# A feed-forward layer cut into four sections instead of two, with output groups between input groups, and 17 instead of 9 of 22 input groups done by seven block products

## The chip, the cores and the metric

The kernel runs on one core of one Trainium2 chip. The metric is the device time of one execution in microseconds (us). One execution was also recorded by the hardware profiler; every row shown below is from that one.

## The reference, cut to what matters

One inference step of a two-layer decoder trunk for 512 prompt tokens and 8 sample tokens (520 columns, D_MODEL 1024), all in float32. Four of its six phases are the same feed-forward half-step with weights of their own:

```python
D_FF = 2816
def swiglu(h, w_in, w_out):
    gate, up = jnp.split(h @ w_in, 2, axis=-1)
    return (jax.nn.silu(gate) * up) @ w_out
# x += 0.5 * swiglu(rms_norm(x), w_in, w_out)      four times: a0, b0, a1, b1
```

The other two phases are a retention/state-space mixer (between a0 and b0) and latent attention (between a1 and b1). The change touches only the four feed-forward phases.

## The kernel before, in words

**Split products.** Every float32 product is made of three matmuls in the reduced type: high part by high part, high by low, low by high. ScalarE makes the high part of a weight chunk (`split_high`, L356), VectorE the low part (`split_low`, L362), each 128 x 512. A chunk is one 256 KB load into a ring of four raw slots; the high and low parts have rings of four of their own. A raw slot is loaded again once its chunk's low part is done; a high slot is written again once TensorE has used the chunk that was there. All weight loads stand in one order on SyncE's queue.

**Input groups.** The 2816 hidden features are 22 groups g of 128. A plain group (`gemm`, L384) takes gate and up of 128 features: 4 chunks, 96 matmuls of 128 x 260. A group in `S_GROUPS` is done by `strassen` (L413 to L447): the product of a 2 x 2 block matrix in seven block products of 12 matmuls each, 84 in all. It needs four sums of weight blocks (`prepare` on VectorE: L910, L913, L914, L919, for which all four raw chunks of the group must have landed), their high and low parts (L662, L899), four sums of the activations made once in each phase (`t_sums` L882 to L887, their parts `t_highs` L652 and `t_lows` L894), and ScalarE copies of partial products out of PSUM (`copy_partial`, L657). TensorE waits inside the group: the third product for the first copy, the fifth for the third copy (`copied`), the seventh for VectorE's first half of `up_second` (L837, `evicted`). Then follow silu (L631), the product with up (L862), and the parts of the hidden tile (L639, L873).

**Output groups.** Each of four output groups (`gemm` on hidden tiles) adds into the residual (`residual`, L961).

**Order.** Two sections of 12 and 10 input groups; after each section its four output groups of 6 and 5 chunks (`mid` and `out`). Groups 0 to 3 are plain, then block-product and plain groups alternate, in hardware loops on TensorE, ScalarE and VectorE (`group_pair`). Accumulators alternate between two sets of four PSUM banks from step to step.

**The start of a phase.** While TensorE does group 0 and group 1, the norm's statistics are made: square root (L617), spread over the partitions by TensorE in the middle of group 1, and copied to `rstd` (L623), without which no group can be scaled out of PSUM. VectorE's list at the start (function `ffn` in the vector block) reads, cut:

```python
for g in range(FIRST_S - 1):
    splits(2 if g else 4)      # chunks of group g + 1
    if g == 0:
        stats((f, "in", 0), nn)
    gate_up(f, g)
    ...
    hidden_low(f, g)
    if g == 1:
        t_sums(f)
```

Each engine runs its list strictly in this written order and waits on semaphores; the order on each engine is written by hand.

Of the kernel before, what the change touches and what calls it, by code (L numbers as in the profile page):

```python
# [10 lines left out]
F32 = mybir.dt.float32  # L11
# [7 lines left out]
P = 128  # L19
# [23 lines left out]
R = 4  # L43
# [7 lines left out]
KFS = max(hi - lo for lo, hi in SECTIONS)  # L51
# [43 lines left out]
def ffn_steps(plan, f):  # L95
    for (lo, hi), name in zip(SECTIONS, ("mid", "out")):
        for g in range(lo, hi):
            plan.step((f, "in", g), 4)
        for g in range(4):
            plan.step((f, name, g), (hi - lo) // 2)  # L100
# [108 lines left out]
def program(nc, io, phases=PHASES):  # L209
# [181 lines left out]
    def count(eng, s, n, i=None, per=1):  # L391

        eng.wait_ge(s, n if i is None else per * i + n)

    def s_index(f, g):

        return len(S_GROUPS) * ffn_index[f] + S_GROUPS.index(g)

    def strassen(pe, f, g, i=None):


        step = (f, "in", g)
        acquire(pe, step, i)
        n, b0, j = plan.first[step], bank0(step), s_index(f, g)
        zb, yb, xb = b0, b0 + 1, b0 + 2

        def ring(c):
            count(pe, w_split, n + c + 1, i, 8)
            return WH[:, (n + c) % R, :], WL[:, (n + c) % R, :]

        def sums(s):
            count(pe, s_low, 3 * j + s + 1, i, 3)
            return SMH[:, s, :], SML[:, s, :]  # L413
# [20 lines left out]
        count(pe, copied, 3 * j + 1, i, 3)  # L434
        product(xb, sums(1), tsum(1), False).then_inc(product_done, 1)
        product(zb, ring(1), block(1, 0), True).then_inc(w_used, 1)
        count(pe, copied, 3 * j + 3, i, 3)
        product(xb, ring(2), tsum(2), False).then_inc(w_used, 1)
        product(yb, sums(2), block(1, 1), False).then_inc(product_done, 1)
        count(pe, evicted, 3 * j + 1, i, 3)  # L440
# [103 lines left out]
    def _(pe):  # L544
        def ffn(f):
# [4 lines left out]
            done = KF * ffn_index[f]  # L550
            h_rhs = lambda k: (HH[:, k, :], HL[:, k, :])
            for (lo, hi), name in zip(SECTIONS, ("mid", "out")):
                g0 = max(lo, FIRST_S)
                for g in range(2 if lo == 0 else lo, g0):
                    gemm(pe, (f, "in", g), 2, KD, x_rhs)
                if lo == 0:
                    pe.wait_ge(x_summed, 8 * (ffn_index[f] + 1))
                with pe.Fori(0, (hi - g0) // 2) as i:
                    strassen(pe, f, g0, i)
                    gemm(pe, (f, "in", g0 + 1), 2, KD, x_rhs, i, 8)  # L560
                for g in range(4):

                    gemm(pe, (f, name, g), 2, hi - lo, h_rhs,
                         before_k=(lambda k: pe.wait_ge(hl_done, done + lo + k + 1)) if g == 0 else None)
# [18 lines left out]
    def _(act):  # L583
# [35 lines left out]
        def stats(step, nn):  # L619
            roots(nn)  # L620
# [5 lines left out]
        def silu(f, g, i=None):  # L626
            if g in S_GROUPS:
                count(act, evicted, 3 * s_index(f, g) + 3, i, 3)
            else:
                wait_free(act, (f, "in", g), i)  # L630
            nc.scalar.activation(SGT[:, g % 2, :], GU[:, g % 2, 0, :], ACT.Silu).then_inc(silu_done, 1)  # L631

        def hidden_high(f, g, i=None):
            n = KF * ffn_index[f] + g + 1
            count(act, hid_done, n, i, 2)
            tile = g - (SECTIONS[1][0] if g >= SECTIONS[1][0] else 0)
            out = HH[:, tile, :] if i is None else HH[:, bass.ds(2 * i + tile, 1), :]
            src = HT[:, g % 2, :] if i is None else HT[:, g % 2:g % 2 + 1, :]
            nc.scalar.activation(out, src, ACT.Copy).then_inc(hh_done, 1)  # L639
# [14 lines left out]
        def copy_partial(f, g, i, bank, out, done, n, per):  # L654

            count(act, done, n, i, per)
            nc.scalar.activation(XU[:, out, :], PS[:, bank0((f, "in", g)) + bank, 0:TH], ACT.Copy).then_inc(copied, 1)  # L657

        def sum_high(f, g, s, i=None):

            count(act, s_sum, 4 * s_index(f, g) + (1, 2, 4)[s], i, 4)
            nc.scalar.activation(SMH[:, s, :], SR[:, s % 2 if s < 2 else 1, :], ACT.Copy).then_inc(s_high, 1)  # L662

        def prepare(f, g, i=None):

            n = plan.first[(f, "in", g)]
            high = lambda c: split_high(act, n + c, i, 6, 8, 2)
            high(0)
            sum_high(f, g, 0, i)
            sum_high(f, g, 1, i)  # L670
            high(1)
            count(act, s_sum, 4 * s_index(f, g) + 3, i, 4)
            high(2)
            sum_high(f, g, 2, i)

        def group_pair(f, g, i=None, before=True, after=True):


            n, j = plan.first[(f, "in", g)], s_index(f, g)
            high = lambda c: split_high(act, n + c, i, 6, 8, 2)  # L680
            high(3)
            copy_partial(f, g, i, 2, 0, w_used, plan.used_through(n), 6)
            if before:
                silu(f, g - 1, i)
            high(4)
            copy_partial(f, g, i, 1, 2, product_done, 3 * j + 1, 3)
            if before:
                hidden_high(f, g - 1, i)
# [2514 lines left out]
```

## Time and profile before

| | us |
|---|---|
| median of 3 runs (2270.8 to 2272.05) | 2271.09 |
| the profiled execution | 2268.74 |
| its span, first to last instruction | 2267.0 |
| TensorE busy | 2207.5 (97%) |
| VectorE busy | 1372.9 (61%) |
| ScalarE busy | 948.8 (42%) |

The profiled execution lies 2.35 us below the median of the runs, and 1.74 us of it lie outside the span. Matmuls are pipelined, so that TensorE is shown busy while it only drains; the distance between the starts of two matmuls is what one costs, not its duration. The names PE, PEld, DVE, ACT, POOL and SP in rows are TensorE's matmuls, its weight loads, VectorE, ScalarE, GpSimd and SyncE.

### The profile page before, as it was taken

What the parts mean: (1) busy time and instruction counts of PE and PEld (TensorE: products, weight loads), DVE (VectorE), ACT (ScalarE), POOL (GpSimd) and SP (SyncE); (2) the same over time, 40 slices, a digit from 0 to 9 for tenths busy, and PEclk for the clock granted to TensorE, in tenths of its full rate; (3) what the DMA queues carried; (4) which work ended last, traced back from release to release, by engine and by line L of the source; (5) the groups of instructions that cost most, each with busy time, mean ns of one, the idle gap of its engine ahead of it and who ended that gap; (6) DMA issues with size and microseconds to landing.
All of it is one profiled execution on the core that took longest, in us unless ns stands there. A gap on an engine that the chain in (4) does not pass through costs nothing.

```text
span 2267.0 us, 48608 instructions
## 1 busy us (share of the span) xinstructions
PE 2207.5 (97%) x19050; PEld 2125.9 (94%) x19050; DVE 1372.9 (61%) x2166; ACT 948.8 (42%) x1669; POOL 171.3 (8%) x243
## 2 busy tenths in 40 slices
PE   9999999999999999999999999999999989999997
PEld 9999999998888999999999999999996689999997
DVE  6754755787436547736746753765557747754754
ACT  6432433562324435423435432443346625432432
POOL 0000002022100010000001000001114501000001
PEclk9999999999999999999999999999999999999999
DMA  4333333233333232333332333333547822333332
GB/s 139 100 95 94 97 97 106 75 101 101 122 119 112 85 103 84 102 90 98 97 94 80 99 97 94 93 101 93 156 146 235 280 85 84 98 96 91 100 95 98
DMA packets 117591, 245.59 MB, mean 108 GB/s; under 512 B 15104, under 2 KB 15376, under 8 KB 116096
## 3 DMA queue, kind: packets, MB, share of 16 engines
q1 hardware_dynamic: 103248, 188.86, 27.6%
q0 software_dynamic: 14048, 54.49, 7.0%
q8 instruction: 111, 1.82, 0.3%
q14 instruction: 40, 0.33, 0.0%
q10 hardware_dynamic: 144, 0.09, 0.0%
HBM read 233.11 MB, written 9.95 MB: 107 GB/s over the span
## 4 chain that ended last, share of the span: by engine, by line
PE 86%; DVE 9%; ACT 2%; issue 2%; DMA 1%; SPq 0%; DVEq 0%; ACTq 0%
PE psum L384 63%; PE psum L428 5%; PE psum L427 5%; PE psum L429 5%; DVE w_low L362 2%; PE psum L2647 1%; PE psum L2662 1%; PE psum L1454 1%; DVE gate_up L827 1%; ACT w_high L356 1%; DVE conv_sum L1884 1%; PE psum L2734 1%; DVE probs_by_key L3074 1%; PE psum L2632 0%; PE psum L2692 0%
## 5 line engine op out<-in xcount | busy, mean ns | idle before, releaser
L362 DVE TENSOR_TENSOR w_low<-w_raw,w_high 128x512 fp32r<-128x512 f32 x703 | 499.3, 720 | 462.2 <-ACT w_high L356 459.7
L356 ACT ACTIVATE w_high<-w_raw 128x512 fp32r<-128x512 f32 x703 | 435.0, 627 | 689.4 <-PE psum L384 533.9
L384 PE MATMUL psum<-x_high,w_high 128*128 128x260 f32 x2688 | 541.6, 283 | 9.3 <-DVE w_low L362 6.0
L384 PE MATMUL psum<-x_low,w_high 128*128 128x260 f32 x2688 | 537.8, 282 | 0.0
L384 PE MATMUL psum<-x_high,w_low 128*128 128x260 f32 x2688 | 537.7, 282 | 0.0
L384 PEld LDWEIGHTS psum<-x_high,w_high 128*128 128x128 f32 x2688 | 414.3, 188 | 16.4 <-issue 4.8
L384 PEld LDWEIGHTS psum<-x_high,w_low 128*128 128x128 f32 x2688 | 414.4, 188 | 0.0
L384 PEld LDWEIGHTS psum<-x_low,w_high 128*128 128x128 f32 x2688 | 414.3, 188 | 0.0
L384 PE MATMUL psum<-hidden_high,w_high 128*128 128x260 f32 x1408 | 282.7, 282 | 0.0
L384 PE MATMUL psum<-hidden_low,w_high 128*128 128x260 f32 x1408 | 282.7, 282 | 0.0
L384 PE MATMUL psum<-hidden_high,w_low 128*128 128x260 f32 x1408 | 282.7, 282 | 0.0
L384 PEld LDWEIGHTS psum<-hidden_high,w_high 128*128 128x128 f32 x1408 | 218.1, 188 | 0.0
L384 PEld LDWEIGHTS psum<-hidden_low,w_high 128*128 128x128 f32 x1408 | 218.1, 188 | 0.0
L384 PEld LDWEIGHTS psum<-hidden_high,w_low 128*128 128x128 f32 x1408 | 218.1, 188 | 0.0
L827 DVE TENSOR_TENSOR gate_up<-psum,rstd 128x520 f32<-128x520 f32 x104 | 67.8, 693 | 79.1 <-PE psum L384 64.8
L1062 POOL TENSOR_TENSOR square_sums<-squares 128x520 f32<-128x520 f32 x6 | 7.9, 1320 | 1415.0 <-ACT squares L607 1415.0
L873 DVE TENSOR_TENSOR hidden_low<-hidden,hidden_high 128x520 f32 (+1 forms) x88 | 61.5, 699 | 62.6 <-ACT hidden_high L639 62.6
L662 ACT ACTIVATE w_sums_high<-w_sums 128x512 fp32r<-128x512 f32 x108 | 67.8, 628 | 63.3 <-DVE w_sums L910 53.8
L639 ACT ACTIVATE hidden_high<-hidden 128x520 f32 (+1 forms) x88 | 56.2, 639 | 87.3 <-DVE hidden L862 86.8
L427 PE MATMUL psum<-x_sums_high,w_high 128*128 128x260 f32 x288 | 81.0, 281 | 8.1 <-ACT partial_products L657 8.1
L961 DVE SCALAR_TENSOR_TENSOR residual<-psum,residual 128x1040 f32<-128x1040 f32 x39 | 48.4, 1241 | 65.5 <-PE psum L384 64.1
L631 ACT ACTIVATE silu_gate<-gate_up 128x520 f32<-128x520 f32 x88 | 55.4, 630 | 77.0 <-DVE gate_up L827 76.7
(438 smaller groups left out, 3510.2 us busy)
## 6 DMA issues: line engine op xcount, KB each, us to landing
w_raw<-in_weights_dram SPq DMA_DIRECT2D x704, 256.0 KB, 2.6
cache_pages<-in_cache_pages_dram POOLq DMA_DIRECT2D x128, 272.0 KB, 4.3
ret_sample_state<-in_state_ret_dram POOLq DMA_DIRECT2D x2, 2048.0 KB, 7.5
out_ret_s_dram<-ret_sample_state POOLq DMA_DIRECT2D x2, 2048.0 KB, 6.6
out_y_dram<-residual SPq DMA_DIRECT2D x8, 260.0 KB, 2.2
ssm_sample_state<-in_state_ssm_dram POOLq DMA_DIRECT2D x2, 1024.0 KB, 5.3
out_ssm_s_dram<-ssm_sample_state POOLq DMA_DIRECT2D x2, 1024.0 KB, 4.8
residual<-in_x_dram SPq DMA_DIRECT2D x3, 520.0 KB, 7.0
```

The costliest lines, as they stand in the source:

```text
L356: nc.scalar.activation(WH[:, slot, :], WRAW[:, slot, :], ACT.Copy).then_inc(w_high, 1)
L362: nc.vector.tensor_tensor(WL[:, slot, :], WRAW[:, slot, :], WH[:, slot, :].bitcast(F32), ALU.subtract).then_inc(w_split, 1)
L384: mm = nc.tensor.matmul(PS[:, b0 + 2 * m + half, 0:cols], w, x[:, half * cols:(half + 1) * cols], start=start, stop=stop)
L427: nc.tensor.matmul(PS[:, bank, 0:TH], wh, xh, start=fresh and kp == 0, stop=False, skip_group_check=True)
L428: nc.tensor.matmul(PS[:, bank, 0:TH], wh, xl, start=False, stop=False, skip_group_check=True)
L429: mm = nc.tensor.matmul(PS[:, bank, 0:TH], wl, xh, start=False, stop=kp == 3, skip_group_check=True)
L631: nc.scalar.activation(SGT[:, g % 2, :], GU[:, g % 2, 0, :], ACT.Silu).then_inc(silu_done, 1)
L639: nc.scalar.activation(out, src, ACT.Copy).then_inc(hh_done, 1)
L662: nc.scalar.activation(SMH[:, s, :], SR[:, s % 2 if s < 2 else 1, :], ACT.Copy).then_inc(s_high, 1)
L827: ins = nc.vector.tensor_tensor(out[:, 2 * m:2 * m + 2, :], acc(step)[:, 2 * m:2 * m + 2, :], halves(RSTD[:]), ALU.mult)
L873: nc.vector.tensor_tensor(out, src, hi.bitcast(F32), ALU.subtract).then_inc(hl_done, 1)
L961: nc.vector.scalar_tensor_tensor(x, acc(step), scale, x, ALU.mult, ALU.add).then_inc(acc_free[plan.set_of[step]], 1)
```

## The change

Four sections of 6, 6, 6 and 4 groups. All groups but 0, 1, 2, 3 and 5 are done by block products (17 of 22). The output groups of a section ("out a", "out b", "out c": 3 chunks each, "out": 2 chunks each) stand between the input groups of the next section; only the last four stand together at the end of the phase. Because output groups come four times instead of twice, there are 16 residual additions in a phase instead of 8. The loops are written out. Each step's side work (splits, sums, copies, evictions) is listed by two functions, `during_s` and `during_plain`, that take the step before, the current and the next one. At the start of a phase the scaling of x (`scaled`, L645) and the activation sums move to earlier places. With P for plain, S for block products, O for an output group, a phase is now: 0P 1P 2P 3P 4S 5P, then S O S S O S O S S O (groups 6 to 11), the same again (12 to 17), S O S O S O S O (18 to 21), O O O O.

```diff
-SECTIONS = ((0, 12), (12, 22))
-FIRST_S = 4
-S_GROUPS = [g for lo, hi in SECTIONS for g in range(max(lo, FIRST_S), hi, 2)]
+SECTIONS = ((0, 6), (6, 12), (12, 18), (18, 22))
+OUT_NAMES = ("out a", "out b", "out c", "out")
+PLAIN_GROUPS = (0, 1, 2, 3, 5)
+S_GROUPS = [g for g in range(KF) if g not in PLAIN_GROUPS]
...
+    order = inner(0, 1, 2, 3, 4, 5)
+    for s in (0, 1):
+        a = SECTIONS[s + 1][0]
+        order += inner(a) + out(s, 0) + inner(a + 1, a + 2) + out(s, 1) + inner(a + 3) + out(s, 2)
+        order += inner(a + 4, a + 5) + out(s, 3)
+    for g in range(4):
+        order += inner(18 + g) + out(2, g)
+    return order + [(f, "out", g) for g in range(4)]
...
 # ScalarE
+        def during_s(prev, cur, nxt):
+            late = kind(prev) == "S"
+            if late:
+                splits(1)
+                silu(prev)
+                copy_product1(cur)
+                split_a21(cur)
+                hidden_high(prev)
+                copy_product5(cur)
+                splits(1)
+                copy_products16(cur)
+                sum_high(cur, 2)
+                splits(3)
+                return
+            splits(1)
+            copy_product1(cur)
+            splits(1)
+            if kind(prev) == "P":
+                silu(prev)
+            copy_product5(cur)
+            if kind(prev) == "P":
+                hidden_high(prev)
+            copy_products16(cur)
+            if kind(nxt) == "S":
+                sum_high(nxt, 0)
+                sum_high(nxt, 1)
+            else:
+                splits(3 if kind(nxt) == "P" else 2)
+        def during_plain(prev, cur, nxt):
+            if prev:
+                silu(prev)
+            splits(1)
+            if prev:
+                hidden_high(prev)
+            sum_high(nxt, 0)
+            sum_high(nxt, 1)
+            splits(1)
+            sum_high(nxt, 2)
+            split_a21(nxt)
...
                 if g == 0:
-                    stats((f, "in", 0), nn)
+                    roots(nn)
+                    wait_stored(act, f)
+                    scaled(f, range(0, 4))
+                    spread(step, nn)
+                    scaled(f, range(4, 8))
                 if g == 1:
-                    scaled(f, range(0, 4))
-                if g == 2:
                     t_highs(f, 0, 1)
-                silu(f, g)
+                silu(step)
...
 # VectorE
+        def during_s(prev, cur, nxt):
+            late = kind(prev) == "S"
+            if late:
+                up_first(prev)
+                sum4(cur)
+                splits(1)
+                product(prev)
+                splits(1)
+                hidden_low(prev)
+                splits(1)
+                sum_low(cur, 2)
+                splits(2)
+                up_second(cur)
+                splits(1)
+                gate(cur)
+                return
+            splits(1)
+            if kind(prev) == "P":
+                gate_up(prev)
             else:
+                residual(prev, prev[2], 0.5)
+            if kind(nxt) == "S":
...
+                sums123(nxt)
+                splits(1)
+                sum_low(nxt, 0)
+                up_second(cur)
+                sum_low(nxt, 1)
+                gate(cur)
+                return
+            splits(1)
...
+            splits(1)
+            up_second(cur)
+            splits(1)
+            gate(cur)
...
+        def during_plain(prev, cur, nxt):
+            if prev:
+                if kind(cur) == "O":
+                    up_first(prev)
+                product(prev)
+            sums123(nxt)
+            splits(1)
+            if prev:
+                hidden_low(prev)
+            sum_low(nxt, 0)
+            sum_low(nxt, 1)
+            sum4(nxt)
+            splits(1)
+            sum_low(nxt, 2)
+            splits(1)
...
-            for g in range(FIRST_S - 1):
+            for g in range(3):
                 splits(2 if g else 4)
                 if g == 0:
-                    stats((f, "in", 0), nn)
+                    stats(step, nn)
-                gate_up(f, g)
-                if g == 2:
+                gate_up(step)
+                if g == 1:
                     t_lows(f, 0, 1)
...
-                hidden_low(f, g)
-                if g == 1:
+                hidden_low(step)
+                if g == 0:
                     t_sums(f)
-                if g == 2:
-                    t_lows(f, 3)
+                if g == 1:
+                    t_lows(f, 2, 3)
```

## Rows read from the trace of the kernel before

**Rows 1.** The page: busy time of each engine (share of the span, instructions).

```profile
PE 2207.5 (97%) x19050; PEld 2125.9 (94%) x19050; DVE 1372.9 (61%) x2166; ACT 948.8 (42%) x1669; POOL 171.3 (8%) x243
```

**Rows 2.** Timeline, phase a0, first matmuls of steps (start, length, engine, line, what).

```profile
71.23 0.40 PE L384 MATMUL psum<-x_high,w_high 128*128 128x260 f32 x2
82.75 0.28 PE L427 MATMUL psum<-x_high,w_high 128*128 128x260 f32 x1
92.73 0.40 PE L384 MATMUL psum<-x_high,w_high 128*128 128x260 f32 x2
147.25 0.40 PE L384 MATMUL psum<-hidden_high,w_high 128*128 128x260 f32 x2
216.37 0.28 PE L427 MATMUL psum<-x_high,w_high 128*128 128x260 f32 x1
```

**Rows 3.** Timeline of TensorE at the start of phase a1, waits in brackets.

```profile
1229.59 0.40 PE L384 MATMUL psum<-x_high,w_high 128*128 128x260 f32 x2
...
1241.66 0.47 PE L384 MATMUL psum<-x_high,w_high 128*128 128x260 f32 x2 [0.71 <-DVE w_low L362]
...
1254.13 0.39 PE L427 MATMUL psum<-x_high,w_high 128*128 128x260 f32 x1 [1.03 <-DVE w_low L362]
...
1257.47 0.38 PE L427 MATMUL psum<-x_sums_high,w_sums_high 128*128 128x260 f32 x1 [0.21 <-ACT partial_products L657]
...
1262.61 0.38 PE L427 MATMUL psum<-x_sums_high,w_high 128*128 128x260 f32 x1 [2.01 <-ACT partial_products L657]
```

**Rows 4.** Timeline of VectorE at the start of phase a1.

```profile
1225.25 0.70 DVE L862 TENSOR_TENSOR hidden<-silu_gate,gate_up 128x520 f32<-128x520 f32 x1 [0.70 <-ACT silu_gate L631]
...
1227.27 1.29 DVE L362 TENSOR_TENSOR w_low<-w_raw,w_high 128x512 fp32r<-128x512 f32 x2
...
1236.09 1.24 DVE L882 TENSOR_TENSOR x_sums<-x_scaled 128x1040 f32<-128x1040 f32 x1
...
1240.83 1.28 DVE L362 TENSOR_TENSOR w_low<-w_raw,w_high 128x512 fp32r<-128x512 f32 x2
```

**Rows 5.** Timeline of ScalarE at the start of phase a1.

```profile
1223.22 1.28 ACT L631 ACT_TABLE_LOAD   x1
1224.58 0.64 ACT L631 ACTIVATE silu_gate<-gate_up 128x520 f32<-128x520 f32 x1
...
1227.57 2.57 ACT L645 ACTIVATE x_scaled<-residual,vectors 128x520 f32<-128x520 f32 x4
```

**Rows 6.** Windows in the mixer phase, and one around the 2.01 us wait.

```profile
566.00:568.00 2.00, 0.00 (x0) 0.00 (x0) 1.93 (x4) 0.46 (x1) 0.60 (x2) 1.00 0.48 202
...
569.00:571.00 2.00, 2.00 (x5) 1.53 (x5) 1.25 (x2) 0.00 (x0) 0.00 (x0) 0.50 0.32 131
...
572.00:574.00 2.00, 2.00 (x18) 1.95 (x17) 0.00 (x0) 1.68 (x2) 0.55 (x1) 1.00 0.33 45
...
1260.00:1270.00 10.00, 7.99 (x68) 7.79 (x67) 7.07 (x12) 4.23 (x9) 0.00 (x0) 1.00 0.42 114
```

The columns are: the window, its length, busy time (and instructions) of PE, PEld, DVE, ACT and POOL, the granted clock (1.00 is 2.4 GHz, 0.50 is 1.2 GHz), the DMA share, GB/s.

**Rows 7.** Timeline: the first matmul after the idle stretch in the mixer phase.

```profile
568.71 1.22 PE L1364 MATMUL psum<-ssm_cum_rows,ssm_cum 128*128 128x512 f32 x2 [3.33 <-DVE ssm_x L2085]
```

**Rows 8.** VectorE: a landing after a split, and sums of a block-product group.

```profile
205.77 0.69 DVE L362 TENSOR_TENSOR w_low<-w_raw,w_high 128x512 fp32r<-128x512 f32 x1 [2.19 <-ACT w_high L356]
209.17 0.69 DVE L910 TENSOR_TENSOR w_sums<-w_raw 128x512 f32<-128x512 f32 x1 [2.71 <-DMA w_raw<-in_weights_dram]
...
210.57 0.69 DVE L914 TENSOR_TENSOR w_raw<-w_raw 128x512 f32<-128x512 f32 x1
211.17 0.68 DVE L362 TENSOR_TENSOR w_low<-w_raw,w_high 128x512 fp32r<-128x512 f32 x1
```

**Rows 9.** Groups by line: VectorE's half-width and widest instructions (count | busy, mean ns).

```profile
L837 DVE TENSOR_TENSOR gate_up<-psum,partial_products 128x260 f32<-128x260 f32 x36 | 15.4, 428 | 6.5 <-PE psum L429 6.3
...
L961 DVE SCALAR_TENSOR_TENSOR residual<-psum,residual 128x1040 f32<-128x1040 f32 x39 | 48.4, 1241 | 65.5 <-PE psum L384 64.1 <-PE psum L2734 1.4
```

**Rows 10.** DMA issues of the page: the slowest load on SyncE's queue (KB, us to landing).

```profile
residual<-in_x_dram SPq DMA_DIRECT2D x3, 520.0 KB, 7.0
```

More of the change, by code:

```diff
@@ L95, in ffn_steps @@
 def ffn_steps(plan, f):
[L96 to L100, printed above, removed]
+    for step in ffn_order(f):
+        lo, hi = SECTIONS[section_of(step)]
+        plan.step(step, 4 if step[1] == "in" else (hi - lo) // 2)
 def make_plan(phases):
@@ L549, in ffn, with pe_steps @@
             gemm(pe, (f, "in", 1), 2, KD, x_rhs, before_k=spread_at(pe, 3, (f, "in", 0), nn))
[L550 to L564, printed above, removed]
+            order = ffn_order(f)
+            pe_steps(order[2:])
+        def pe_steps(steps):
+            for step in steps:
+                f = step[0]
+                if kind(step) == "P":
+                    gemm(pe, step, 2, KD, x_rhs)
+                elif kind(step) == "S":
+                    if step[2] == S_GROUPS[0]:
+                        pe.wait_ge(x_summed, 8 * (ffn_index[f] + 1))
+                    strassen(pe, step)
+                else:
+                    lo, hi = SECTIONS[section_of(step)]
+                    t0, n0 = hidden_tile(lo), KF * ffn_index[f] + lo
+                    gemm(pe, step, 2, hi - lo, lambda k: (HH[:, t0 + k, :], HL[:, t0 + k, :]),
+                         before_k=(lambda k: pe.wait_ge(hl_done, n0 + k + 1)) if step[2] == 0 else None)
         pe.wait_ge(table_set, 2)
@@ L664, in prepare, with copy_product1 @@
[L664 to L688, printed above, removed]
-            copy_partial(f, g, i, 2, 1, product_done, 3 * j + 2, 3)
-            high(5)
-            high(6)
-            high(7)
-            silu(f, g, i)
-            hidden_high(f, g, i)
-            if after:
-                prepare(f, g + 2, i)
+        def copy_product1(step):
+            act.wait_ge(w_used, plan.used_through(plan.first[step]))
+            nc.scalar.activation(XU[:, 0, :], PS[:, bank0(step) + 2, 0:TH], ACT.Copy).then_inc(copied, 1)
@@ L900, in sum_low, with raw @@
                                     ALU.subtract).then_inc(s_low, 1)
-        def prepare(f, g, i=None):
-            n, j = plan.first[(f, "in", g)], s_index(f, g)
-            a11, a12, a21, a22 = (WRAW[:, (n + c) % R, :] for c in range(4))
-            loaded = lambda c: count(dve, w_loaded[(n + c) % R], 16 * ((n + c) // R + 1), i, 32)
-            low = lambda c: split_low(dve, n + c, i, 8)
-            loaded(2)
-            loaded(3)
+        def raw(step, c):
+            n = plan.first[step] + c
+            dve.wait_ge(w_loaded[n % R], 16 * (n // R + 1))
+            return WRAW[:, n % R, :]
@@ L965, in ffn @@
             nn = nn_of[f]
[L966 removed]
+            order = ffn_order(f)
+            for g in range(3):
+                step = order[g]
                 splits(2 if g else 4)
                 if g == 0:
[L969 to L971 removed]
+                    stats(step, nn)
+                gate_up(step)
+                if g == 1:
                     t_lows(f, 0, 1)
@@ L974, in ffn @@
                     splits(1)
-                product(f, g)
-                if g == 2:
-                    t_lows(f, 2)
+                product(step)
                 if g:
@@ L1090, in ffn_chunks @@
     out = []
-    for lo, hi in SECTIONS:
-        out += [blocks[g] if g in S_GROUPS else plain[g] for g in range(lo, hi)]
-        out.append(b[:, lo // 2:hi // 2].reshape(-1, P, CW))
+    for _, name, g in ffn_order(None):
+        if name == "in":
+            out.append(blocks[g] if g in S_GROUPS else plain[g])
+        else:
+            lo, hi = SECTIONS[OUT_NAMES.index(name)]
+            out.append(b[g, lo // 2:hi // 2])
     return out
```

312 lines of the change are left out of this document (139 added, 173 removed).

## The prediction, made before the changed kernel was run

> **What bounds the kernel now.** I read the busy times first: TensorE is busy for 97% of the span [rows 1], so a gain must come out of its list or out of its waits. That figure only says where to look, since matmuls overlap; what a step costs is the distance to the start of the next step, and I took it from the timeline [rows 2]. The reader is to see three lengths there. A plain input group lasts 82.75 - 71.23 = 11.52 us for 96 matmuls, a block-product group 92.73 - 82.75 = 9.98 us for 84, and the 24 chunks of four output groups 216.37 - 147.25 = 69.12 us, 2.88 each. Between such steps no row shows a wait: in the body of a phase TensorE sets the pace. The exception is the start of a phase, where TensorE waits four times [rows 3]: 0.71 us before group 3, 1.03 before group 4 (the first by block products), 0.21 and 2.01 inside it, 3.96 in all. The other phases show the same four, up to 0.4 us apart. The side work at that place I read from the timelines of VectorE and ScalarE [rows 4, 5].
>
> **The change, part by part.** *Fewer matmuls.* Eight more groups in a phase go by block products: 8 x (11.52 - 9.98) = 12.3 us less. Output chunks stay 44 in a phase at 2.88, so cutting them into more groups costs TensorE nothing. The eight extra residual additions, 1.24 us each [rows 9], fall on VectorE during the next input group.
>
> *The start of a phase.* Group 2 cannot start before VectorE has split its first chunk. Before, that split comes right after group 0's hidden tile, at 1227.27, and the sums of x come later, after group 1's. In the new list the four sums stand after group 0's hidden tile, ahead of the split of group 2. They take from 1236.09 to the next split at 1240.83, 4.74 us [rows 4]. Group 0's hidden tile also comes later: ScalarE now does four scalings before the first silu. These four take 2.57 us, and the table load of 1.28 that precedes the silu directly (1223.22 to 1224.58 without a gap) moves behind them [rows 5]; with the overlap of neighbours that is 2.5 us for silu, product, hidden tile and everything behind it on VectorE. There was some room: TensorE starts 0.83 us after the start of a pair of splits (1240.83 to 1241.66), so group 2 could have begun at 1228.10 and began at 1229.59 [rows 3, 4], 1.49 later. The new wait is 4.74 + 2.5 - 1.49 = 5.75 us in each phase. Behind the late split stand group 1's eviction and the low parts of the sums; they delay nothing more, because the third chunk of group 2 is needed only two chunks, 5.76 us, after its start, and VectorE has five instructions of 0.6 to 1.24 ahead of it, about 4.8 in all. Bounds: 3.25 if the later silu were covered, 6.8 if group 0's table load, copies and hand-overs slip by another 1 us.
>
> *The clock after that wait.* After 3.33 us of idling in the mixer phase [rows 7] the granted clock stood at 0.50 and was back at 1.00 by 572, at most 3.3 us after the first matmul [rows 6]. Across the 2.01 us wait in a feed-forward phase it stayed at 1.00 [rows 6]. A wait of 5.75 is nearer to the first. At half the clock 3.3 us do the work of 1.65; bounds 0 and 1.65, and I take 1.4. The Trainium skill (TensorE: Matmul & The Clock Gate, "HAM oscillation — how this bites in real kernels") says that a wait between bursts of matmuls puts the array back to the half clock, so that the next burst begins slow; by that rule alone the term would be near its upper end, by the row of the 2.01 us wait it would be 0. The trace agrees with the rule once, in the mixer phase, and in no feed-forward phase.
>
> *The rest of the start.* Group 3's chunks are now split before group 2 ends, since the sums are out of the way: the 0.71 us goes. Group 4's start waits for its last raw chunk and three sums; the low parts of the sums of x have left this place, so its 1.03 shrinks to some 0.2. But ScalarE now makes the high part of a third chunk before its first copy (one pass of about 0.5), so the wait before the third product grows from 0.21 to 0.7; the wait before the fifth, for the eviction, silu and hidden tile of group 3, goes from 2.01 to about 1.4. Together 2.3 for 3.25: 1.0 us less. Bounds: nothing gained, and all 3.25 gained.
>
> *Two block-product groups in a row* (four times in a phase) are the step that the old list never had. While the first runs, VectorE must split its last chunk, add a residual, and make the sums of the second, for which the second's last raw chunk must have landed. Count from the first group's start. The last chunk's high slot is free only at 0; high and low part end at about 1.5. The load that this frees lands 2.71 later [rows 8], at 4.2; the residual fits between. Two sums take 1.40, a third 0.60, a split 0.60, a low part 0.60 [rows 8]: VectorE reaches the half-width addition at 7.4. It can't be earlier than the fifth product's end, 5 x 1.43 = 7.1. It takes 0.43 [rows 9] and frees the seventh product at 7.9, which TensorE reaches at 6 x 1.43 = 8.6: room of 0.6 us. In the second group the same addition stands behind two splits that wait for TensorE's fourth product (5.7), and comes at 7.4 again. So I cost the pairs at nothing, covered by 0.6 us; with that cover gone each pair pays one for one what is late. The upper bound comes from the slowest load on the same queue, 7.0 [rows 10]: 4.3 later, 3.7 per pair.
>
> *VectorE as a whole.* A block-product group is 15 full-width instructions at 0.60 to 0.70 from start to start [rows 8] and three half-width ones of 0.43 [rows 9], 10.3 to 11.8 us against 9.98 on TensorE: more than it. An output group is three splits and one residual, about 3.3 against 8.64. Over S O S S O that makes 37 to 42 of 47.2 us. It fits because output groups stand between, and VectorE carries its backlog into them. Bounds for the whole body: 0, and 0.7 us per pair if the hand-overs are slower than in the old list.
>
> *Elsewhere.* At the end of a phase the output groups now last 5.76 us instead of 14.4. VectorE has a residual, two low parts of x and two splits for each, at most 3 x 1.24 + 2 x 0.69 = 5.1 [rows 8, 9], so they stay covered. Loop heads go; no row shows that they cost anything.
>
> **The sum, per phase:** -12.3 + 5.75 + 1.4 - 0.7 - 1.0 = -6.9 us. Four phases: -27.5. The profiled execution of 2268.74 us would become 2241.2; it lies 2.35 below the median of the runs, so the median becomes 2271.1 - 27.5 = 2243.6; I say 2243. The bounds of these terms taken together: -12.3 + 3.25 + 0 - 0.7 - 3.25 = -13.0 (2219), and -12.3 + 6.8 + 1.65 - 0.7 + 0 + 4 x 0.7 = -1.8 (2264).
>
> **The rivals.**
> - *The clock holds* through the wait at group 2, as it held through the 2.01 us wait: -6.9 - 1.4 = -8.3 per phase, 2238. Against it stands that the wait is longer than the one that dropped the clock.
> - *Group 2 doesn't wait*: the sums are hidden. -12.3 - 0.7 - 1.0 = -14.0 per phase, 2215. For it speaks that VectorE stood idle here before (0.70 us ahead of the product [rows 4]); against it that VectorE's list is strict and 4.74 us of sums stand in front of a split with room for 1.49.
> - *The pairs slip a little*: 0.3 to 0.7 us in each of 16 pairs, and some at the single groups, 5 to 20 us: 2248 to 2263. For it: room of only 0.6.
> - *The pairs' loads are late* (the one that ends slower): the second group's last chunk lands so late that the first's seventh product waits. Place: each pair, on VectorE ahead of the half-width addition. To cost the 27.5 us that I forecast, 16 pairs must lose 1.7 each, 0.6 + 1.7 = 2.3 beyond the plan: landings of 5.0 instead of 2.71. At 7.0 it would be 3.7 x 16 = 59 us, 2302. Against it: in this stretch nothing else is being loaded, and 2.71 is among the longer waits that the old list shows.
> - *The change does not do what it says* (a saved matmul isn't saved time) can't be: both lengths are seen side by side in one stretch.
>
> **How the numbers follow.** The forecast has 0.55 with its own range of 2240 to 2248; the clock holds 0.20; the pairs slip 0.12; group 2 doesn't wait 0.07; late loads 0.06. The 8-in-10 range is 2226 to 2260: it leaves out late loads, most of "doesn't wait" and the end of the slipping pairs. 0.2% (4.5 us) is about what a measurement of this kernel can tell from no change. Faster by more takes all cases but late loads and a corner of it: 0.91; within it 0.03; slower 0.06.
>
> **What would show it.** Right: groups by block products 9.98 long also when two stand in a row; a wait of about 5.5 us of TensorE on a split (L362's successor) before group 2 in each phase, with x_sums instructions ahead of that split on VectorE; a granted clock below 1.00 just behind it; waits inside group 4 of about 2.3. Wrong: no wait at group 2 (the order at the start misread); waits on VectorE's addition before seventh products (the pairs); a plain sum of steps that doesn't add up to the phase, which would mean a wait that I don't list. The prediction fails most easily at the pairs, where 0.6 us of room is worked out from hand-overs of about 0.2 us each.

## The result, and the profile after

The changed kernel takes 2248.66 us (median of 4 runs, 2243.94 to 2250.7), the kernel before 2271.57 beside it: ratio 0.9889, 95% interval 0.9871 to 0.9907, 22.9 us less. The forecast was 2243, 27.5 less. The profiled execution below is the fastest of the four: 2243.94, 24.8 below the profiled one of before. The four runs order by their mean granted clock: 2243.94 at 0.991, 2247.04 at 0.989, 2250.29 at 0.987, 2250.7 at 0.986.

The page's busy times, against [rows 1]: TensorE has 384 matmuls fewer and is still busy for 97% of its span, VectorE went from 61 to 71%.

```profile
PE 2165.0 (97%) x18666; PEld 2083.4 (93%) x18666; DVE 1582.0 (71%) x2518; ACT 1035.6 (46%) x1861; POOL 171.2 (8%) x243
```

The body of a phase: TensorE's timeline in a0, the first matmuls of four steps, against [rows 2].

```profile
87.85 0.28 PE L457 MATMUL psum<-x_high,w_high 128*128 128x260 f32 x1
...
97.83 0.40 PE L415 MATMUL psum<-hidden_high,w_high 128*128 128x260 f32 x2
...
106.47 0.28 PE L457 MATMUL psum<-x_high,w_high 128*128 128x260 f32 x1
...
126.44 0.40 PE L415 MATMUL psum<-hidden_high,w_high 128*128 128x260 f32 x2
```

A block-product group is 97.83 - 87.85 = 9.98 us, an output group of three chunks 8.64, a pair of block-product groups 126.44 - 106.47 = 19.97, twice 9.98. 15 of the 16 pairs are that long to 0.05 us.

The start of a phase: TensorE's timeline in a1, waits in brackets, against [rows 3].

```profile
1200.18 0.51 PE L415 MATMUL psum<-x_high,w_high 128*128 128x260 f32 x2 [0.82 <-DVE x_low L841]
...
1221.27 0.77 PE L415 MATMUL psum<-x_high,w_high 128*128 128x260 f32 x2 [5.61 <-DVE w_low L393]
...
1250.89 0.39 PE L457 MATMUL psum<-x_sums_high,w_sums_high 128*128 128x260 f32 x1 [0.60 <-ACT partial_products L689]
...
1255.07 0.39 PE L457 MATMUL psum<-x_sums_high,w_high 128*128 128x260 f32 x1 [1.06 <-ACT partial_products L697]
```

The wait of 0.71 before group 3 is gone. A wait of 5.61 before group 2 is new (5.32, 5.68 and 5.68 in the other phases), and so is one of 0.82 inside group 0, which began at 1190.56. The reason for the first stands in VectorE's timeline of the same place, against [rows 4]:

```profile
1213.68 0.70 DVE L899 TENSOR_TENSOR hidden<-silu_gate,gate_up 128x520 f32<-128x520 f32 x1 [3.13 <-ACT silu_gate L667]
...
1215.71 1.23 DVE L916 TENSOR_TENSOR x_sums<-x_scaled 128x1040 f32<-128x1040 f32 x1
...
1219.28 1.24 DVE L921 TENSOR_TENSOR x_sums<-x_scaled,x_sums 128x1040 f32<-128x1040 f32 x1
1220.44 1.28 DVE L393 TENSOR_TENSOR w_low<-w_raw,w_high 128x512 fp32r<-128x512 f32 x2
```

The four sums occupy 1215.71 to 1220.44, 4.73 us, ahead of the split that TensorE waits for; ahead of them VectorE idles 3.13 us for the silu.

The granted clock there, in windows (columns as in [rows 6]):

```profile
1219.00:1221.00 2.00, 0.00 (x0) 0.00 (x0) 1.97 (x3) 0.20 (x1) 0.00 (x0) 0.80 0.00 0
1221.00:1223.00 2.00, 1.73 (x8) 1.76 (x9) 2.00 (x5) 0.03 (x1) 0.00 (x0) 0.50 0.15 47
1223.00:1225.00 2.00, 2.00 (x11) 2.00 (x11) 2.00 (x2) 2.00 (x3) 0.00 (x0) 0.50 0.57 215
1225.00:1227.00 2.00, 2.00 (x11) 2.00 (x10) 1.45 (x3) 0.61 (x2) 0.00 (x0) 0.50 0.01 3
1227.00:1229.00 2.00, 2.00 (x19) 2.00 (x18) 1.32 (x3) 2.00 (x4) 0.00 (x0) 1.00 0.48 128
```

The clock falls 1.1 us before the wait ends and is back at 1227.0, so that TensorE works at 1.2 GHz for almost six microseconds: 11 matmuls in two microseconds, 19 once the clock is back. The stretch at half is 6.8 us long in a1, b0 and b1 and 3.4 in a0, and part of it lies in the wait. Over windows of 1 us, busy time times the missing share of the clock adds up to 2.87 us here, and to 1.52, 1.59 and 2.45 in a0, b0 and b1: 8.4 us. In a second profiled execution (2246.5 us of span) it is 2.27, 2.95, 1.98 and 2.12: 9.3.

The wait inside group 0 comes from the end of the phase before. VectorE's timeline there:

```profile
1186.29 0.68 DVE L393 TENSOR_TENSOR w_low<-w_raw,w_high 128x512 fp32r<-128x512 f32 x1
1186.90 1.23 DVE L1031 SCALAR_TENSOR_TENSOR residual<-psum,residual 128x1040 f32<-128x1040 f32 x1
1189.79 1.41 DVE L393 TENSOR_TENSOR w_low<-w_raw,w_high 128x512 fp32r<-128x512 f32 x1 [1.66 <-ACT w_high L387]
1191.12 2.48 DVE L841 SCALAR_TENSOR_TENSOR x_low<-residual,vectors,x_high 128x520 fp32r<-128x520 f32 x2
1193.51 0.68 DVE L393 TENSOR_TENSOR w_low<-w_raw,w_high 128x512 fp32r<-128x512 f32 x1
1194.11 1.23 DVE L1031 SCALAR_TENSOR_TENSOR residual<-psum,residual 128x1040 f32<-128x1040 f32 x1
```

and GpSimd's, which adds the squares of the same tiles:

```profile
1189.31 1.33 POOL L1120 TENSOR_TENSOR square_sums<-square_sums,squares 128x520 f32<-128x520 f32 x1 [4.17 <-ACT squares L639]
1190.72 1.64 POOL L1123 TENSOR_TENSOR square_sums<-square_sums,squares 128x520 f32<-128x520 f32 x1
```

From one residual to the next VectorE needs 1194.11 - 1186.90 = 7.2 us, TensorE 5.76. The split at 1189.79 takes 1.41 where its neighbours take 0.68, and a low part of x 1.24: both lie beside GpSimd's additions. So VectorE falls behind by 1.4 per output group, and the low parts of x come late.

The list of TensorE's waits of the whole program, cut, adds it up (total, times, longest):

```profile
PE psum L457 <- ACT partial_products L697: 4.3, 4, 1.1
...
PE psum L457 <- ACT partial_products L689: 2.4, 4, 0.6
PE psum L415 <- DVE x_low L841: 2.4, 3, 0.8
...
PE psum L457 <- DVE gate_up L874: 1.4, 1, 1.4
...
PE psum L457 <- DVE w_low L393: 0.5, 1, 0.5
```

The 1.4 is one pair in b1, where the raw chunk came late; by the starts of its steps this pair lasts 21.65 us for 19.96, 1.7 more (VectorE's timeline there):

```profile
2102.08 1.24 DVE L1031 SCALAR_TENSOR_TENSOR residual<-psum,residual 128x1040 f32<-128x1040 f32 x1
2106.99 0.69 DVE L946 TENSOR_TENSOR w_sums<-w_raw 128x512 f32<-128x512 f32 x1 [3.67 <-DMA w_raw<-in_weights_dram]
```

### The profile page after: what moved, and what is told of

The parts are those of the page before. It is cut to its first block, busy times and chain, and to the rows that moved or that the text cites. A ratio compares the mean times of both kernels' runs of the same rounds, so it can differ in the third digit from the quotient of the medians.

```text
span 2242.2 us, 47354 instructions
## 1 busy us (share of the span) xinstructions
PE 2165.0 (97%) x18666; PEld 2083.4 (93%) x18666; DVE 1582.0 (71%) x2518; ACT 1035.6 (46%) x1861; POOL 171.2 (8%) x243
## 4 chain that ended last, share of the span: by engine, by line
PE 79%; DVE 13%; ACT 4%; issue 2%; DMA 1%; SPq 0%; DVEq 0%; ACTq 0%
PE psum L415 43%; PE psum L458 10%; PE psum L459 10%; PE psum L457 10%; DVE w_low L393 3%; DVE x_low L841 1%; PE psum L2705 1%; ACT w_high L387 1%; PE psum L2720 1%; ACT x_scaled L678 1%; PE psum L1512 1%; DVE residual L1031 1%; DMA w_raw<-in_weights_dram 1%; DVE conv_sum L1942 1%; PE psum L2792 1%
## 5 line engine op out<-in xcount | busy, mean ns | idle before, releaser
L415 PE MATMUL psum<-x_low,w_high 128*128 128x260 f32 x1664 | 334.9, 283 | 0.0
L415 PE MATMUL psum<-x_high,w_low 128*128 128x260 f32 x1664 | 334.6, 283 | 0.0
L415 PEld LDWEIGHTS psum<-x_high,w_high 128*128 128x128 f32 x1664 | 259.1, 190 | 40.3 <-issue 24.7
L415 PEld LDWEIGHTS psum<-x_low,w_high 128*128 128x128 f32 x1664 | 258.9, 190 | 0.0
L415 PEld LDWEIGHTS psum<-x_high,w_low 128*128 128x128 f32 x1664 | 258.5, 190 | 0.0
L457 PE MATMUL psum<-x_sums_high,w_sums_high 128*128 128x260 f32 x544 | 152.7, 281 | 2.4 <-ACT partial_products L689 2.4
L459 PE MATMUL psum<-x_sums_high,w_low 128*128 128x260 f32 x544 | 153.7, 282 | 0.0
L459 PE MATMUL psum<-x_sums_high,w_sums_low 128*128 128x260 f32 x544 | 153.7, 282 | 0.0
L458 PE MATMUL psum<-x_sums_low,w_sums_high 128*128 128x260 f32 x544 | 153.3, 282 | 0.0
L458 PE MATMUL psum<-x_sums_low,w_high 128*128 128x260 f32 x544 | 153.3, 282 | 0.0
```

The costliest lines, as they stand in the source:

```text
L415: mm = nc.tensor.matmul(PS[:, b0 + 2 * m + half, 0:cols], w, x[:, half * cols:(half + 1) * cols], start=start, stop=stop)
L457: nc.tensor.matmul(PS[:, bank, 0:TH], wh, xh, start=fresh and kp == 0, stop=False, skip_group_check=True)
L458: nc.tensor.matmul(PS[:, bank, 0:TH], wh, xl, start=False, stop=False, skip_group_check=True)
L459: mm = nc.tensor.matmul(PS[:, bank, 0:TH], wl, xh, start=False, stop=kp == 3, skip_group_check=True)
```

## The experiments

Eleven kernels in three groups; each group shared a chip with runs of the kernel before. One of them is the changed kernel once more, and differences in microseconds are taken from it unless another is named; across groups the ratios to the kernel before are the safer figures.

**The changed kernel again.**

> The changed kernel once more, beside the experiments on one chip: 2249 us if the half clock behind the wait is as long as in the median of its first four runs, 2244 if as in the profiled one.

2248.57 us (2246.9 to 2252.26), ratio 0.9898 [0.9879, 0.9916].

**The body alone.** The start of a phase as before: scalings, sums, highs and lows each one group later.

```diff
                 if g == 0:
-                    roots(nn)
-                    wait_stored(act, f)
+                    stats(step, nn)
+                if g == 1:
                     scaled(f, range(0, 4))
-                    spread(step, nn)
-                    scaled(f, range(4, 8))
-                if g == 1:
+                if g == 2:
                     t_highs(f, 0, 1)
                 silu(step)
...
-                if g == 0:
+                if g == 1:
                     t_sums(f)
```

> The new body (four sections, output groups among input groups, pairs of block-product groups) with the start of each phase in the old order: scalings during group 1, sums after group 1, their high and low parts during group 2. Theory: the body alone gives -12.3 us per phase, the end of a phase gives back about 0.85, and the old start adds nothing but its old 4.0 us of waits, so 4 x -11.45 = -45.8 us against the kernel before, about 2225 us; no wait of over 2 us before group 2, and the granted clock near 0.995 on the mean. Rival: a part of the body's gain was never there and the new start costs less than the trace makes it: 2240 us or more.

2223.3 us (2220.65 to 2226.39), ratio 0.9784 [0.9766, 0.9802], 49.1 below the kernel before. The theory holds, the rival does not. All of the body's gain was there (that 49.1 meets the 49.2 of the sum is partly luck: this trace also holds 2.7 us of new waits on the low part of x and 1.6 lost in its pairs, against 2.3 less waiting inside group 4), and the new start of a phase costs 2248.57 - 2223.3 = 25.3 us, half of it. The granted clock stays at 1.00 in groups 0 to 4 of every phase. Its waits on splits are those of before: group 3 in the first line (which also holds other stages), group 4's start in the second.

```profile
PE psum L415 <- DVE w_low L393: 6.5, 8, 1.4
PE psum L457 <- DVE w_low L393: 4.3, 4, 1.2
```

**Sums behind the splits of group 2** (they stood behind group 0's hidden tile on VectorE).

```diff
-                splits(2 if g else 4)
+                splits((4, 3, 2)[g])
...
+                if g == 1:
+                    t_sums(f)
                 gate_up(step)
...
-                if g == 0:
-                    t_sums(f)
```

> The changed kernel, with the four sums of the inputs moved behind the first three weight splits for group 2 on VectorE (and the third split moved ahead on ScalarE). Theory: the wait of 5.3 to 5.7 us before group 2 is the 4.7 us of sums in front of the split, so it falls below 1 us, the clock stays at full speed behind it, and the two together give 4 x about 6.9 = 27 us: about 2221 us. Rival: the wait is mostly the late silu, so it stays at 2.5 us or more: 2232 us or more. Second rival: the sums only move the wait to the third weight chunk of group 2 or to group 3: 2235 us or more.

2240.42 us (2236.34 to 2243.59), ratio 0.9858 [0.984, 0.9876]. The second rival is right. The wait before group 2 falls to 0.9, so it was the sums; but they then stand in front of group 1's eviction, its silu and the split of the fourth chunk, and TensorE waits there, inside group 2:

```profile
1215.74 0.48 PE L415 MATMUL psum<-x_high,w_high 128*128 128x260 f32 x2 [0.87 <-DVE w_low L393]
...
1227.63 0.51 PE L415 MATMUL psum<-x_high,w_high 128*128 128x260 f32 x2 [3.01 <-DVE w_low L393]
```

After this 3.01 the clock stayed at 1.00 in a1, and after 3.22 in a0; after 3.22 in b0 and 3.21 in b1 it stood at half, which cost 3.1 and 1.7. The 8.2 us saved are about 4.9 of waits on splits (26.8 to 21.9 for the program) and the rest clock.

**TensorE busy through the wait.** The results of the added matmuls are overwritten by group 2.

```diff
+    def fill_wait(pe, step):
+        def fill(k):
+            for _ in range(42 if k == 0 else 0):
+                nc.tensor.matmul(PS[:, bank0(step), 0:TH], XH[:, 0, 0:P], XH[:, 0, 0:TH], start=True, stop=True)
+        return fill
...
-                    gemm(pe, step, 2, KD, x_rhs)
+                    gemm(pe, step, 2, KD, x_rhs, before_k=fill_wait(pe, step) if step[2] == 2 else None)
```

> The changed kernel with 42 matmuls of 128x128 by 260 columns added on TensorE at the start of group 2, into the banks that group 2 then overwrites: TensorE works through most of the wait, which itself stays. Theory: the granted clock stays at 1.00 behind the wait; the half clock costs 1.6 to 2.9 us per phase in the trace, 8.9 us in all, so 2240 us. Rival: the half clock costs only what the forecast allowed, 1.4 per phase: 2243 us. Second rival: the added matmuls take longer than the wait and delay group 2: 2249 us or more.

2241.24 us (2237.29 to 2241.83), ratio 0.9853 [0.9835, 0.9871]: 7.3 less, with group 2 no earlier for its splits. From its start to that of group 3, group 2 lasts 11.62 us in every phase, against 13.26 to 14.23 in the changed kernel again: 8.0 in all. The windows behind the wait in a1:

```profile
1217.00:1219.00 2.00, 1.82 (x16) 1.61 (x14) 1.97 (x3) 0.38 (x1) 0.00 (x0) 1.00 0.00 0
1219.00:1221.00 2.00, 1.64 (x13) 1.65 (x14) 2.00 (x4) 0.00 (x0) 0.00 (x0) 1.00 0.21 32
1221.00:1223.00 2.00, 2.00 (x19) 2.00 (x18) 2.00 (x3) 1.85 (x3) 0.00 (x0) 1.00 0.60 230
```

The clock holds at 1.00, in all four phases. So the half clock by itself costs about 7 to 9 us, more than the forecast's 5.6.

**Scalings early, sums in the old place** (the body alone, plus the scalings ahead of the first silu; the lines are against the body alone).

```diff
                 if g == 0:
-                    stats(step, nn)
-                if g == 1:
+                    roots(nn)
+                    wait_stored(act, f)
                     scaled(f, range(0, 4))
+                    spread(step, nn)
+                    scaled(f, range(4, 8))
...
-                if g == 1:
-                    scaled(f, range(4, 6))
...
-                if g == 1:
-                    scaled(f, range(6, 8))
```

> The new body with the sums, their high and low parts in the old places, but all scalings ahead of the first silu, as in the changed kernel. Theory: it is the sums in front of the split that make most of the wait before group 2; the late silu alone leaves 0.9 us of it, too short for the clock to fall, as in the run with the sums behind the splits: 2223.3 + 4 x 0.9 = 2227 us. Rival: the clock falls there all the same in some phases: 2231 us or more. Second rival: the scalings done earlier free ScalarE in group 1 and give it back: 2223 us or less.

2228.31 us (2225.55 to 2231.16), ratio 0.9804 [0.979, 0.9817]: 5.0 above the body alone, its clock at 1.00 in groups 0 to 4 of every phase. The two intervals overlap, but the traces agree with the medians: group 1 lasts 13.0 us here and 12.0 with the body alone, 4.2 for the four phases, and group 2 another 0.5. The theory's 4 lies within the spread. So of the 25 us of the new start the late silu alone makes about 5; the other 20, taken as the rest, go to the sums and their parts one group earlier, with the half clock behind the wait.

**The second split ahead of the squares**, at the end of a phase.

```diff
                 if nn + 1 < NN or g < 3:
+                    splits(1)
                     wait_free(act, (f, "out", g))
                 squares(nn + 1, g)
                 if nn + 1 < NN:
-                    splits(1)
                     highs(nn + 1, g)
-                elif g < 3:
-                    splits(1)
```

> The changed kernel with one edit at the end of a phase: in the last four output groups ScalarE makes the high parts of both weight chunks ahead of the squares, not one ahead and one behind. Theory: VectorE's chain per output group is 7.2 us against 5.76 on TensorE because its split waits for a high part that stands behind the squares; without that the chain is under 5.8, the waits of 0.76 to 0.82 us on the low part of x at the start of the next phase go, and the wait at the final norm falls from 1.66 to about 1.2: -2.8 us, 2246 us. Rival: the chain is bound by the squares and the high parts of x themselves, and the waits stay: 2249 us.

2241.98 us (2239.91 to 2243.21), ratio 0.9859 [0.9844, 0.9873]. The three waits on the low part of x that follow the end of a phase are gone, 2.4 us of the list (one of 0.7 at the program's start, with no phase before it, stays). The chain is only down to 6.5 us, not under 5.8 as the theory had it: a low part of x takes 1.5 beside GpSimd.

```profile
1189.94 1.23 DVE L1029 SCALAR_TENSOR_TENSOR residual<-psum,residual 128x1040 f32<-128x1040 f32 x1
...
1192.93 3.02 DVE L839 SCALAR_TENSOR_TENSOR x_low<-residual,vectors,x_high 128x520 fp32r<-128x520 f32 x2 [1.16 <-ACT x_high L644]
...
1196.48 1.23 DVE L1029 SCALAR_TENSOR_TENSOR residual<-psum,residual 128x1040 f32<-128x1040 f32 x1
```

The medians differ by 6.6; what is more than 2.4 has no wait in the list, and the two profiled executions differ in how long the clock stood at half in other stages (12.4 us of cost against 14.7 in all). I put only the 2.4 down to the edit; the rest stays open.

**Without GpSimd's additions.**

```diff
                 else:
-                    pool.wait_ge(squares_added, q - 4)
-                    nc.gpsimd.tensor_tensor(SQS[:], SQS[:], SQT[:, 0, :], ALU.add).then_inc(sum_half, 1)
-                    ...
-                    nc.gpsimd.tensor_tensor(SQS[:], SQS[:], SQT[:, 1, :], ALU.add).then_inc(squares_added, 1)
+                    pool.sem_inc(squares_added, 1)
```

> The changed kernel without GpSimd's additions of the squares of tiles 2 to 7 (six of its seven additions at the end of every phase; the norms are then taken from the squares of two tiles alone). Theory: beside these additions VectorE's split takes 1.39 us where it takes 0.69 elsewhere, and its low parts of x 1.2 to 1.5 where 0.71; without them the chain per output group falls from 7.2 to about 5.8 us and the waits of about 0.8 us on the low part of x at the start of a phase go, with the order of the splits as it was. Total 2243 to 2246 us. Rival: the order of the splits on ScalarE alone makes the chain long; it stays above 6.5 us and the waits stay: 2248 us.

2245.4 us (2244.08 to 2249.86), ratio 0.9881 [0.9866, 0.9896]. VectorE's timeline at the same place, with the order of the splits as in the changed kernel:

```profile
1187.86 1.23 DVE L1031 SCALAR_TENSOR_TENSOR residual<-psum,residual 128x1040 f32<-128x1040 f32 x1
1190.75 0.69 DVE L393 TENSOR_TENSOR w_low<-w_raw,w_high 128x512 fp32r<-128x512 f32 x1 [1.66 <-ACT w_high L387]
1191.37 1.43 DVE L841 SCALAR_TENSOR_TENSOR x_low<-residual,vectors,x_high 128x520 fp32r<-128x520 f32 x2
1192.72 0.69 DVE L393 TENSOR_TENSOR w_low<-w_raw,w_high 128x512 fp32r<-128x512 f32 x1
1193.44 1.24 DVE L1031 SCALAR_TENSOR_TENSOR residual<-psum,residual 128x1040 f32<-128x1040 f32 x1
```

The same idle of 1.66, the same order, but the split takes 0.69 and a low part of x 0.71; the chain is 5.6 and the three waits on the low part of x are gone. The time alone would not show it, since the interval overlaps that of the changed kernel again; the rows do. The theory holds: the additions lengthen VectorE's work, and the order of the splits is only another way to make room.

**One and two copies in the pairs**, ahead of the half-width addition of the first group (the second kernel has `range(2)`).

```diff
                 sum_low(nxt, 0)
+                for m in range(1):
+                    link(nc.vector.tensor_copy(SPARE[:], SMH[:, 0, :].bitcast(F32)))
                 up_second(cur)
```

> The changed kernel with one VectorE copy of 128x512 (about 0.6 us with its wait) added in front of the second-half sum of the first group of each pair of block-product groups, 16 in all. Theory: this place has 0.6 us of room, as the forecast took it, so at most 0.2 us of each copy shows: within 3 us of the changed kernel. Rival: the place has no room, and every copy shows: +10 us.

> The same with two copies (about 1.2 us with their waits). Theory: 0.6 us of room, then 0.6 us shows in each of 16 pairs: +10 us against the changed kernel. Rival with no room: +19 us. Rival with room above 1.2: nothing.

2254.38 us (2251.45 to 2256.45), ratio 0.9911 [0.9898, 0.9924], and 2261.13 (2257.64 to 2268.24), ratio 0.9951 [0.9935, 0.9967]. A copy takes 0.46 with its hand-over, not 0.6. The 16 pairs last 20.38 us on the mean with one and 20.89 with two, against 20.07 in the changed kernel (its late load among them): 0.31 and 0.82 more, of 0.46 and 0.92 put in. So the pairs hid 0.1 to 0.15 of it. The theories' 0.6 of room falls, and the rival "no room" is nearly right; its +10 and +19 were too high, since a copy is shorter than assumed. Two copies cost 12.6 us between the medians, near the 10 of their theory, but by a short copy of which little is hidden, not by a long one half hidden. The trace of two copies names the place:

```profile
PE psum L458 <- DVE gate_up L875: 10.5, 16, 1.2
```

In the changed kernel's first pair (timelines of VectorE and of TensorE):

```profile
114.44 0.42 DVE L874 TENSOR_TENSOR gate_up<-psum,partial_products 128x260 f32<-128x260 f32 x1
...
115.03 0.28 PE L457 MATMUL psum<-x_sums_high,w_high 128*128 128x260 f32 x1
```

From the end of the addition to the start of the seventh product it is 0.17 here, and 0.12 to 0.52 in the other pairs without a late load, 0.34 on the mean; 0.06 of it passes even where TensorE waits for the addition.

**Two edits together**: sums behind the splits and the second split first; then the body alone and the second split first.

> The sums behind the splits and the splits ahead of the squares together. Theory: the two gains are in different places and add: 2221 - 2.8 = about 2218 us, faster than both kernels. Rival: the earlier split at the end of a phase is hidden by the wait before group 2 alone, and adds nothing: 2221 us.

> The new body with the old start of a phase, and the high parts of both weight chunks ahead of the squares in the last four output groups. Theory: the two add up: 2223.3 less the 2.7 us of waits on the low part of x, about 2219 us, and faster than both kernels. Rival: at the old start the wait at the beginning of a phase has room behind it and nothing is gained: 2223 us.

2235.75 us (2233.67 to 2241.8), ratio 0.9832 [0.9819, 0.9845]: the first theory's 2218 fails because the sums' own run did not reach 2221; below that run it lies 4.7, so the two seem to add, though the intervals just overlap. The waits of 3.01 to 3.25 inside group 2 left the clock at half in all four phases here, where it was two of four in the sums' own run. The second pair gives 2220.9 us (2220.4 to 2223.41), ratio 0.9771 [0.9758, 0.9785]: the lowest median of the study, 27.7 us below the changed one. Its 2.4 us below the body alone are the size of the waits removed, but the two intervals overlap.

## Why the prediction came out as it did

The terms of the sum, for four phases, in the profiled executions (us):

| term | forecast | measured |
|---|---|---|
| eight more groups by block products | -49.2 | -49.2 (9.98 each); the body alone -49.1 in all, with other terms in it |
| wait before group 2 | +23.0 | +22.3 |
| half clock behind it | +5.6 | +8.4 (9.3 in the second profile; 7.3 by the busy wait) |
| group 3's wait | -2.8 | -2.5 |
| group 4's waits | -4.0 | -6.2 (13.3 to 7.1) |
| end of a phase | 0 | +2.4 |
| pairs | 0 | +1.8, nearly all of it one late load |
| sum | -27.4 (given as -27.5) | -23.0 |

The profiled executions differ by 24.8. The remaining 1.8 is about the clock in the mixer and attention phases, which cost 4.9 us in the profile of before and 3.0 here.

- *Fewer matmuls.* Right to the hundredth, also in pairs; the body alone shows the gain in the time.
- *The start of a phase.* Right: 5.75 was forecast and 5.3 to 5.7 came, by the cause named. The two shares were taken apart: the sums behind the split take the wait away (and make another), the scalings alone cost 5 us in all. The rival "group 2 doesn't wait" is out.
- *The clock.* The mechanism was right and the term mis-sized. The forecast let the half clock last at most 3.3 us, as in the one stretch of the mixer phase [rows 6], with 1.65 as the upper bound of its price; it lasted 3 to 6 us of work and cost 1.5 to 2.95 per phase. That stretch was not the only one in the trace of before: the clock also stood at half for 3.4 us from 524.1, behind a wait of 0.76, and for 3.4 us from 1821.2, one microsecond behind a wait of 2.02, so that the two chosen rows were not all that bore on the term. But none of these three was longer than 3.4 us, so a stretch of 6.8 could not be read there. The cost also varies between the two profiled executions of one kernel, and the four times of the changed kernel, 6.8 us apart, stand in the order of their clocks. The rival "the clock holds" is out. The Trainium skill's rule (TensorE: Matmul & The Clock Gate, "HAM oscillation — how this bites in real kernels") speaks for a slow burst after each such wait; the trace agrees in all four phases.
- *The rest of the start.* Group 3's wait went. Group 4's three waits came to 1.7 to 2.2 per phase for 2.3 forecast: the splits ahead of its start no longer make TensorE wait in most phases, and the fifth product's 1.06 was put at 1.4.
- *The pairs.* Their cost of nothing was right and the cover behind it wrong: 0.6 us of room was forecast and 0.17 is there in the pair looked at, since the half-width addition comes 7.97 us after the pair's start and not 7.4. The work between the first sum and the addition takes the 3.2 that was planned; the sums begin at 4.76 instead of 4.2, when the load has landed. "The pairs slip a little", which has the measured time in its range, is not what happened: in the profiled execution 15 of 16 pairs lost nothing. The rival "the pairs' loads are late" happened once in 16: the sums began 4.9 us after the residual ahead of them, where 2.9 to 3.3 is usual, and the pair was 1.7 longer. With the busy wait one other pair was 2.0 longer, with the changed kernel again one 0.8, and with the body alone none more than 0.7. Why a load is late now and then stays open.
- *Elsewhere, the end of a phase.* This step failed. "At most 3 x 1.24 + 2 x 0.69 = 5.1 [rows 8, 9], so they stay covered" counted VectorE's work by rows of other places, and left out the 1.66 that it waits for the high part behind the squares. At this place a split takes 1.4 and a low part of x 1.24, 7.2 in all against 5.76. In the trace of before the same wait and the same lengths stand beside GpSimd's additions, under output groups of 14.4 us that covered them (its rows are below). The Trainium skill (SBUF — State Buffer, "SBUF: two separate sides") says that VectorE instructions with two SBUF inputs and GpSimd instructions that read SBUF share ports, which one of them holds for a whole instruction while the other waits. The trace agrees that the two hinder each other: without the additions the split is back from 1.41 to 0.69 and the low part from 1.24 to 0.71. That ports are the reason no run here shows.

VectorE in the trace of before, at the end of phase b0:

```profile
1176.94 1.24 DVE L961 SCALAR_TENSOR_TENSOR residual<-psum,residual 128x1040 f32<-128x1040 f32 x1 [1.46 <-PE psum L384]
1179.85 1.41 DVE L362 TENSOR_TENSOR w_low<-w_raw,w_high 128x512 fp32r<-128x512 f32 x1 [1.66 <-ACT w_high L356]
1181.18 2.47 DVE L804 SCALAR_TENSOR_TENSOR x_low<-residual,vectors,x_high 128x520 fp32r<-128x520 f32 x2
1183.58 1.28 DVE L362 TENSOR_TENSOR w_low<-w_raw,w_high 128x512 fp32r<-128x512 f32 x2
```

So in the profiled executions the terms come to a gain 4.4 us smaller than forecast: the clock (+2.8; +3.7 in the second profile), the end of the phase (+2.4), the pairs (+1.8) and group 3 (+0.3), less the better waits in group 4 (-2.2) and before group 2 (-0.7). That the misses partly cancel is luck. The medians are 22.9 apart, 4.6 less than forecast, and 2248.66 lies just above the range of 2240 to 2248 that had 0.55. The change as a whole is two edits of opposite sign, -49 and +25.

## What to carry to other kernels

Price an instruction by rows from its own place and with its neighbours, not by the same instruction elsewhere, and when a step is shortened that covered side work, walk the side work's whole chain with its waits against the new length. An early start for side work is no gain where it stands ahead of what the bottleneck needs next: run each edit of a bundled change alone, since a gain of 49 can hide a loss of 25. A cover worked out from hand-overs should be measured by putting work into it.

## What the runs showed of the hardware

- After idling for 5.3 to 5.7 us at the start of a phase TensorE restarted at a granted clock of 0.50 in every phase of the six traces that have this wait, and stayed there for 3 to 6 us of work; with matmuls put into the wait it stayed at 1.00. After waits of 3.0 to 3.25 us inside group 2 it stood at half in two phases of four (the sums behind the splits) and in four of four (both edits), and after the 3.3 us wait of the mixer phase in all thirteen traces.
- Beside GpSimd's additions of 128x520 (1.31 to 1.65 us each) VectorE's split of 128x512 took 1.39 to 1.48 instead of 0.69, and its low part of x 1.24 to 1.5 instead of 0.71.
